# Turning a block's weights ahead of the next block's scores in a two-layer decoder step

## The chip, the cores and the metric

One core of a Trainium2 chip runs the whole program. The metric is the device time of one execution in microseconds, as the median of several runs; lower is better. The engines are TensorE (PE for its matrix products, PEld for its weight loads), VectorE (DVE), ScalarE (ACT), GpSimd (POOL) and SyncE (SP), which issues most transfers.

## What is computed

The reference is one inference step of a two-layer decoder on 1024 prompt rows and 8 single rows with a past of 1024 (the samples). Each layer normalises x, projects it (h @ w_in) into a pooling part and q, k, v of four heads, attends, projects back, and then runs a convolution-gated feed-forward part. What matters here is the attention of the prompt, with two score maps per head:

```python
def diff_core(q, k, v, q_pos, k_pos, lam):
    s = jnp.einsum('bqhcd,bkhcd->bhcqk', q, k).astype(F32) * (HEAD_DIM ** -0.5)
    mask = k_pos[None, :] <= q_pos[:, None]
    s = jnp.where(mask, s, -jnp.inf)
    p = jax.nn.softmax(s, axis=-1)
    a = p[:, :, 0] - lam * p[:, :, 1]
    return jnp.einsum('bhqk,bkhe->bqhe', a.astype(v.dtype), v)
```

HEAD_DIM is 64, a block has 128 queries, and a prompt has 8 blocks.

## The kernel before

The program is written engine by engine; every order of work and every semaphore wait is set by hand, and each engine runs its list in that order. A layer has three stages: the input projections, four heads of attention (about 85 us each, the last one longer), and the feed-forward part.

**A head.** Its eight blocks are taken in the order 7, 0, 6, 1, 5, 2, 4, 3 (`ORDER`), one in each of the steps s = 0 to 7. Block i sees i + 1 blocks of 128 keys, so its two score maps are 128 x 128(i + 1). Narrow and wide blocks alternate: in step s the scores of step s + 1 are made, so the even steps make narrow ones (1, 2, 3 and 4 blocks of keys) and the odd ones wide ones (7, 6, 5, and in step 7 the 8 blocks of the next head).

**Who does what for one block.** PE makes the two score maps in the PSUM banks 2-3 and 4-5 (`scores`, lines 549 to 567: products of 64 rows at L560 and L564, then a causal mask of 128 rows at L566). DVE takes the row maxima (`maxima`, L1930), ACT the two exponentials (`exps`, L1418 and L1421), and DVE puts them together into the weights in SBUF (`combine`, L1939 to L1946), which frees bank 4. PE then turns the weights in rounds of up to four blocks into bank 6 (`turn_p`, L574; a turn is one product of the weights with the identity; two instructions), ACT copies each round to SBUF (`take_p`, L1436), and PE multiplies them by v (`weigh`, L585) into bank 7. The result is squared by ACT (`square`, L1430), POOL makes the factor (`rms`, L1149, L1151), DVE scales by it (`normalise`, L1956), PE turns it into bank 6 (`turn_out`, L596) one step later, and ACT takes it (`take_out`, L1447; L1444 in the last head).

**What fills the gaps.** Between these PE runs products that have no part in the chain: in the first three heads the projections of the next head (`in_slice`, L484), in the last head those of the output (`out_slice`, L499), in the banks 0 and 1 by turns. `FILL` and `FILL_OUT` say how many of them a step has; a third of them stands behind each of the two places in a step, the rest behind `turn_out`. In step 7 a third is 6 products.

**The samples.** Each head also has the 8 samples: POOL multiplies gathered cache pages (L1174) and DVE sums them (`k_sum`, L1971); in step 4 PE turns these sums (L618), in steps 5 and 6 it weighs gathered pages of v (`sample_values`, L642), whose transfers POOL starts (L1166), and in step 7 of the first three heads it spreads the next head's q over the partitions (`spread_q`, L546) through bank 6 and bank 7.

**The order on the other engines in a step.** Neither list is touched by the change:

```python
# ACT, step s                      # DVE, step s
square(it, s - 1)                  maxima(*after)
take_p(it, s, 0)                   normalise(it, s - 1)
exps(*after)                       combine(*after)
...
take_p(it, s, 1)                   k_sum(it, b)
...
take_out(it, s - 1)
```

`after` is the block of the next step. So the exponentials of the next block stand behind the copy of this block's first round on ACT, `take_out` stands behind these exponentials, and `normalise` stands behind the next block's maxima on DVE.

Of the kernel before, what the change touches and what calls it, by code (L numbers as in the profile page):

```python
# [63 lines left out]
def rounds(i):  # L64
    return [list(range(a, min(a + 4, i + 1))) for a in range(0, i + 1, 4)]


def third(s, counts):

    return 0 if counts is FILL_OUT and s == 0 else counts[s] // 3  # L70
# [66 lines left out]
def hybrid_decoder_kernel(nc, x_prompt, x_sample, cache_k, cache_v, state_pool, state_conv, page_table, norm1_g, w_in,  # L137
# [4 lines left out]
    with ExitStack() as ctx:  # L142
# [178 lines left out]
        def claim(pe, name, b):  # L321
            USE[name] = (b, USES[b])
            if USES[b]:
                pe.wait_ge(bank_free[b], USES[b])
            USES[b] += 1
            return b
# [10 lines left out]
        def freed(eng, name):  # L337
            b, n = USE[name]
            eng.wait_ge(bank_free[b], n + 1)
# [76 lines left out]
        def _(pe):  # L416
# [93 lines left out]
            def slices(l, items, banks):  # L510
                for kind, n, t in items:
                    yield from (in_slice if kind == "in" else out_slice)(l, n, t, next(banks))

            def take(fill, n):
                for _ in range(n):
                    next(fill, None)
# [21 lines left out]
            def small_k(it):  # L538
                b = claim(pe, ("ks", it), 6)
                pe.transpose(bank[0:8, b, 0:P], k_buf[it % 2][:, SEQ:T], ident).then_inc(bank_full[b], 1)  # L540
# [8 lines left out]
            def scores(it, s):  # L549
                i = ORDER[s]  # L550
                q, k = q_buf[it % 2], k_buf[it % 2]
                for c in range(2):
                    claim(pe, ("s", it, s, c), 2 + 2 * c)
                if s == 0:
                    pe.wait_ge(roped, it * 2 + 2)
                halves = [(2 + 2 * c, slice(c * HEAD_DIM, (c + 1) * HEAD_DIM)) for c in range(2)]
                for n, at in enumerate(range(0, i * P, 512)):
                    w = min(512, i * P - at)
                    for b, rows in halves:
                        pe.matmul(bank[:, b + n, 0:w], q[rows, i * P:(i + 1) * P], k[rows, at:at + w],  # L560
                                  start=True, stop=True)
                last = [bank[:, b + i // 4, (i % 4) * P:(i % 4 + 1) * P] for b, _ in halves]
                for c, (b, rows) in enumerate(halves):
                    pe.matmul(last[c], q[rows, i * P:(i + 1) * P], k[rows, i * P:(i + 1) * P], start=True, stop=False)  # L564
                for c, (b, rows) in enumerate(halves):
                    pe.matmul(last[c], mask[:, 0, :], mask[:, 1, :], start=False, stop=True  # L566
                              ).then_inc(bank_full[b], 1)

            def turn_p(it, s, r):
                b = claim(pe, ("p", it, s, r), 6)  # L570
                if r == 0:
                    freed(pe, ("s", it, s, 1))
                for n, i in enumerate(rounds(ORDER[s])[r]):
                    ins = pe.transpose(bank[:, b, n * P:(n + 1) * P], probs[s % 2][:, i * P:(i + 1) * P], ident)  # L574
                ins.then_inc(bank_full[b], 1)
# [13 lines left out]
            def turn_out(it, n):  # L589
                b = claim(pe, ("to", it, n), 6)  # L590
                if n == QT_N:
                    freed(pe, ("so", it))
                    pe.transpose(bank[:, b, 0:8], o_norm8, ident[0:8, 0:8]).then_inc(bank_full[b], 1)
                else:
                    freed(pe, ("o", it, n))
                    pe.transpose(bank[:, b, 0:P], o_norm, ident).then_inc(bank_full[b], 1)  # L596

            def turn_v(it, r, b):
                claim(pe, ("vt", it, r), b)
                l, h = it // N_HEADS, it % N_HEADS  # L600
                if r == 0:
                    freed(pe, ("g", l, U_V(h), NT - 1))
                for a in range(4):
                    i = 4 * r + a
                    ins = pe.transpose(bank[:, b, a * P:(a + 1) * P], v_T[:, i * P:(i + 1) * P], ident)
                ins.then_inc(bank_full[b], 1)

            def small_v(it):
                b = claim(pe, ("vs", it), 6)
                pe.transpose(bank[0:16, b, 0:P], v_T[:, SEQ:T + 8], ident).then_inc(bank_full[b], 1)  # L610

            def turn_sample_scores(it):
                for r in range(2):
                    b = claim(pe, ("ss", it, r), 7 - r)
                    if r == 0:
                        pe.wait_ge(k_red, (it + 1) * DEC_BATCH)
                    for a in range(4):
                        ins = pe.transpose(bank[0:16, b, a * P:(a + 1) * P], s_score[:, :, :, 4 * r + a], ident)  # L618
                    ins.then_inc(bank_full[b], 1)
                b = claim(pe, ("ss", it, 2), 7)  # L620
                pe.wait_ge(qk_done, it + 1)
                pe.matmul(bank[0:16, b, 0:1], comp8, ones[:, 0:1], start=True, stop=True).then_inc(bank_full[b], 1)

            def sample_weights(it):
                b = claim(pe, ("sw", it), 6)
                pe.wait_ge(soft_sel, it + 1)
                for j in range(N_PAGES):
                    ins = pe.matmul(bank[:, b, j * 8:j * 8 + 8], soft[:, j * P:(j + 1) * P], sel8,
                                    start=True, stop=True)
                ins.then_inc(bank_full[b], 1)  # L630
# [37 lines left out]
            for l in range(DEPTH):  # L668
# [48 lines left out]
                it = l * N_HEADS  # L717
# [12 lines left out]
                for h in range(N_HEADS):  # L730
                    it = l * N_HEADS + h
                    final = h == N_HEADS - 1
                    if final:
                        fill = slices(l, [("out", m, t) for m in range(KC) for t in range(NT)], banks)
                        counts = FILL_OUT
                    else:
                        fill = slices(l, [("in", u(h + 1), t) for u in (U_K, U_Q, U_V) for t in range(NT)], banks)
                        counts = FILL
                    for s in range(QT_N):
                        part = third(s, counts)  # L740
                        if s + 1 < QT_N:
                            scores(it, s + 1)
                        elif not final:
                            scores(it + 1, 0)
                        turn_p(it, s, 0)
                        take(fill, part)
                        if len(rounds(ORDER[s])) > 1:
                            turn_p(it, s, 1)
                        take(fill, part)
                        if s >= 1:  # L750
                            turn_out(it, s - 1)
                        elif h:
                            turn_out(it - 1, QT_N - 1)
                        if s == 0:
                            turn_v(it, 0, 7)
                            turn_v(it, 1, 6)
                            small_v(it)
                            if h:
                                turn_out(it - 1, QT_N)
                        if s == 4:  # L760
                            turn_sample_scores(it)
                        if s == 5:
                            sample_weights(it)
                            if not final:
                                turn_k(it + 1, 0, 6)
                                turn_k(it + 1, 1, 7)
                        if s == 7 and not final:
                            spread_q(it + 1, 0, 6)
                            spread_q(it + 1, 1, 7)
                            small_k(it + 1)  # L770
                        if final and s == 0:
                            weigh(it, s)
                        if s == 5:
                            sample_values(it, 0)
                        take(fill, counts[s] - 2 * part)
                        if s == 6:
                            sample_values(it, 1)
                        if s == 7:
                            sample_out(it, next(banks))
                        if not (final and s == 0):  # L780
                            weigh(it, s)


                it = l * N_HEADS + N_HEADS - 1
# [1432 lines left out]
```

## Time and profile before

| | us |
|---|---|
| median of 3 runs | 2738.33 |
| their lowest and highest | 2734.73, 2739.3 |
| the profiled execution | 2739.19 |
| its span, first to last instruction | 2737.4 |

The mean granted clock of TensorE in the profiled execution was 0.962 of full speed. The page gives the busy time of each engine, the chain of work that ended last, and groups of instructions; the trace behind it can be asked for waits, for stretches and for single instructions in order of time. Start times count from the first instruction. An instruction's duration on PE runs to its modelled end, so consecutive products overlap: how far their starts lie apart is what they cost.

### The profile page before, as it was taken

The page shows a single profiled execution, that of the slowest core. Times are in us where ns is not written, and L with a number is a line of the kernel's source. Part 1 is how long each engine was busy: PE and PEld are TensorE (multiplying, and loading weights), DVE is VectorE, ACT ScalarE, POOL GpSimd, SP SyncE. Part 2 cuts the span into 40 slices and gives each one's busy share as a digit, 9 for nine tenths or more (in the row PEclk, how much of TensorE's full clock was granted, in tenths as well). Part 3 has the DMA queues.
Part 4 walks back from the last instruction along what each step waited for, and adds up shares of the span by engine and source line. Part 5 has one row for each costly group of instructions (what it writes and reads, how often), then busy time and mean ns, then how long its engine had stood idle before and what let it go on. Part 6 is the DMA issues. An engine that isn't in the chain of part 4 may idle for free.

```text
span 2737.4 us, 41317 instructions
## 1 busy us (share of the span) xinstructions
PE 2545.7 (93%) x16556; PEld 2381.9 (87%) x16556; DVE 1417.5 (52%) x1845; ACT 740.3 (27%) x1409; POOL 794.9 (29%) x537
## 2 busy tenths in 40 slices
PE   6889898989999999999988899899899999999996
PEld 6777777889999999999887777688899999999995
DVE  6554555265454544444565556545455454544445
ACT  3134433242111111111142444424211111111112
POOL 1254555312122212222122566442221122112220
PEclk8999999999999999999999999899999999999998
DMA  4334444201111111111113455421111111111101
GB/s 144 104 102 148 147 143 149 85 25 46 46 46 46 46 46 46 46 46 41 63 40 105 140 153 159 162 82 47 47 47 46 46 46 46 46 46 46 46 23 62
DMA packets 78359, 205.96 MB, mean 75 GB/s; under 512 B 9146, under 2 KB 31100, under 8 KB 77994
## 3 DMA queue, kind: packets, MB, share of 16 engines
q1 hardware_dynamic: 57018, 136.27, 15.0%
q0 software_dynamic: 18496, 67.58, 7.9%
q8 instruction: 67, 1.10, 0.2%
q10 hardware_dynamic: 2752, 0.80, 0.1%
q14 instruction: 26, 0.21, 0.0%
HBM read 176.63 MB, written 19.98 MB: 72 GB/s over the span
## 4 chain that ended last, share of the span: by engine, by line
PE 80%; DVE 8%; issue 4%; ACT 3%; POOL 3%; DMA 2%; ACTq 1%; DVEq 0%; POOLq 0%; SPq 0%
PE bank L820 35%; PE bank L843 19%; PE bank L484 8%; PE bank L499 5%; PE bank L585 2%; PE bank L560 2%; DMA arena<-in_cache_v,idx 1%; PE bank L877 1%; DVE arena L1898 1%; PE bank L642 1%; PE bank L664 1%; POOL arena L1166 1%; PE bank L574 1%; POOL w_lo L1131 1%; DVE arena L1783 1%
## 5 line engine op out<-in xcount | busy, mean ns | idle before, releaser
L1249 POOL TENSOR_TENSOR w_lo<-w_raw,w_hi 128x1024 fp32r<-128x1024 f32 x126 | 309.8, 2459 | 1166.5 <-ACT w_hi L1619 1166.5
L2126 DVE TENSOR_TENSOR resid<-bank,resid 128x1032 f32<-128x1032 f32 x336 | 414.2, 1233 | 94.6 <-PE bank L843 94.6
L820 PE MATMUL bank<-act_hi,w_hi 128*128 128x344 f32 x2016 | 433.8, 324 | 3.7 <-DVE arena L2101 3.7
L820 PE MATMUL bank<-act_hi,w_lo 128*128 128x344 f32 x2016 | 428.2, 321 | 0.0
L820 PE MATMUL bank<-act_lo,w_hi 128*128 128x344 f32 x2016 | 426.8, 320 | 0.0
L820 PEld LDWEIGHTS bank<-act_hi,w_hi 128*128 128x128 f32 x2016 | 336.2, 189 | 7.5 <-issue 3.8
L820 PEld LDWEIGHTS bank<-act_hi,w_lo 128*128 128x128 f32 x2016 | 341.1, 189 | 0.0
L820 PEld LDWEIGHTS bank<-act_lo,w_hi 128*128 128x128 f32 x2016 | 338.4, 189 | 0.0
L843 PE MATMUL bank<-gate_hi,w_hi 128*128 128x344 f32 x1008 | 237.2, 344 | 8.3 <-DVE gate_lo L2119 8.3
L484 PE MATMUL bank<-act_hi,w_hi 128*128 128x344 f32 x672 | 225.6, 336 | 14.2 <-DVE arena L1879 14.2
L484 PE MATMUL bank<-act_hi,w_lo 128*128 128x344 f32 x672 | 225.0, 335 | 0.0
L484 PE MATMUL bank<-act_lo,w_hi 128*128 128x344 f32 x672 | 220.9, 329 | 0.0
L843 PE MATMUL bank<-gate_hi,w_lo 128*128 128x344 f32 x1008 | 214.3, 321 | 0.0
L843 PE MATMUL bank<-gate_lo,w_hi 128*128 128x344 f32 x1008 | 214.1, 321 | 0.0
L1131 POOL TENSOR_TENSOR w_lo<-w_raw,w_hi 128x1024 fp32r<-128x1024 f32 (+1 forms) x56 | 137.2, 2451 | 211.0 <-ACT w_hi L1288 210.8
L843 PEld LDWEIGHTS bank<-gate_hi,w_hi 128*128 128x128 f32 x1008 | 156.3, 190 | 44.0 <-DVE resid L2126 24.1
L1930 DVE TENSOR_REDUCE stat<-bank 128x1 f32<-128x128 f32 (+7 forms) x128 | 90.9, 752 | 197.5 <-PE bank L566 197.5
L1631 ACT ACTIVATE arena<-arena 128x1024 f32<-128x1024 f32 x44 | 46.7, 1062 | 528.0 <-DVE arena L2109 528.0
L843 PEld LDWEIGHTS bank<-gate_hi,w_lo 128*128 128x128 f32 x1008 | 170.0, 189 | 0.0
L843 PEld LDWEIGHTS bank<-gate_lo,w_hi 128*128 128x128 f32 x1008 | 169.9, 189 | 0.0
L2117 DVE TENSOR_TENSOR arena<-bank,arena 128x1032 f32<-128x1032 f32 x44 | 54.4, 1236 | 207.3 <-PE bank L820 207.0
L1174 POOL TENSOR_TENSOR arena<-arena 128x1024 f32<-128x1024 f32 x64 | 152.1, 2381 | 20.8 <-ACT arena L1411 19.4
(238 smaller groups left out, 4032.3 us busy)
## 6 DMA issues: line engine op xcount, KB each, us to landing
w_raw<-in_w_up SPq DMA_DIRECT2D x88, 512.0 KB, 3.9
w_raw<-in_w_down SPq DMA_DIRECT2D x44, 512.0 KB, 3.4
w_raw<-in_w_in SPq DMA_DIRECT2D x32, 512.0 KB, 3.4
out<-arena SPq DMA_DIRECT2D x24, 512.0 KB, 3.3
arena<-arena SPq DMA_DIRECT2D x64, 129.0 KB, 2.4
w_raw<-in_w_out SPq DMA_DIRECT2D x16, 448.0 KB, 3.5
mix_spill<-arena SPq DMA_DIRECT2D x12, 516.0 KB, 3.5
arena<-in_x_prompt SPq DMA_DIRECT2D x8, 512.0 KB, 11.4
```

The source lines that it names most:

```text
L484: ins = pe.matmul(bank[:, b, 0:TW], w_of(w, l, n, k), x[:, k, cols(t)], start=(k == 0 and m == 0), stop=(k == KC - 1 and m == 2))
L499: ins = pe.matmul(bank[:, b, 0:TW], w_of(w, l, U_O + m, c), x[:, c, cols(t)], start=(c == 0 and a == 0), stop=(c == KC - 2 and a == 2))
L560: pe.matmul(bank[:, b + n, 0:w], q[rows, i * P:(i + 1) * P], k[rows, at:at + w], start=True, stop=True)
L585: ins = pe.matmul(bank[:, b, 0:P], a_T[:, r, n * P:(n + 1) * P], v_tok[:, j, :], start=(j == 0), stop=(j == i))
L820: ins = pe.matmul(grp(u[0])[:, t, :], w_of(w, l, n, k), x[:, k, cols(t)], start=(k == 0 and n_ == 0), stop=(k == KC - 1 and n_ == 2))
L843: ins = pe.matmul(grp(u[0])[:, t, :], w_of(w, l, n, m), x[:, cols(t)], start=(n_ == 0), stop=(n_ == 2))
L1131: pool.tensor_tensor(w_lo[:, slot, 0:width], w_raw[:, r % SLOTS, 0:width], w_hi[:, slot, 0:width].bitcast(F32), ALU.subtract).then_inc(w_l ...
L1174: pool.tensor_tensor(kp, kp, q_row, ALU.mult).then_inc(k_mul, 1)
L1249: pool.tensor_tensor(w_lo[:, slot, :], w_raw[:, r % SLOTS, 0:1024], w_hi[:, slot, :].bitcast(F32), ALU.subtract).then_inc(w_lo_done, 1)
L1930: dve.tensor_reduce(stat[:, s % 2, c:c + 1], flat(b)[:, 0:width], AX_X, ALU.min).then_inc(att_bias, 1)
L2117: dve.tensor_tensor(tiles(gate), grp(u[0]), tiles(gate), ALU.mult).then_inc(fg_free[u[0]], 1)
L2126: dve.tensor_tensor(tiles(resid[:, m, :]), grp(u[0]), tiles(resid[:, m, :]), ALU.add).then_inc(fg_free[u[0]], 1)
```

## The change

In each step of a head the call that turns the first round of the current block's weights is moved from behind the next block's scores to in front of them. The two waits that the two calls have in common (the banks of the scores are free, the weights are combined) are the same semaphore; the turn also claims bank 6. In step 7 of a last head no scores follow, and nothing moves. The lists of the other engines stay as they are.

```diff
                     for s in range(QT_N):
                         part = third(s, counts)
+                        turn_p(it, s, 0)
                         if s + 1 < QT_N:
                             scores(it, s + 1)
                         elif not final:
                             scores(it + 1, 0)
-                        turn_p(it, s, 0)
                         take(fill, part)
                         if len(rounds(ORDER[s])) > 1:
                             turn_p(it, s, 1)
```

## Rows read from the trace of the kernel before

**Rows 1.** The page's part 4: shares of the chain that ended last, by engine.

```profile
PE 80%; DVE 8%; issue 4%; ACT 3%; POOL 3%; DMA 2%; ACTq 1%; DVEq 0%; POOLq 0%; SPq 0%
```

**Rows 2.** PE's waits, layer 0's heads: line, releaser, total us, times, longest.

```profile
PE bank L618 <- DVE parts_b L1971: 7.7, 4, 2.1
PE bank L642 <- DMA arena<-in_cache_v,idx: 6.7, 3, 2.3
...
PE bank L546 <- ACT arena L1447: 2.5, 3, 0.8
PE bank L499 <- DVE resid L2001: 2.5, 2, 2.2
...
PE bank L596 <- DVE arena L1956: 1.2, 3, 0.4
```

**Rows 3.** Timeline of step 7, layer 0's first head: start, length, engine, line.

```profile
236.89 1.77 PE L560 MATMUL bank<-arena 64*128 64x512 f32 x8
...
238.94 0.61 PE L574 MATMUL bank<-con,arena 128*128 128x128 f32 x4
239.09 2.36 DVE L1930 TENSOR_REDUCE stat<-bank 128x1 f32<-128x1024 f32 x2 [4.61 <-PE bank L566]
...
240.34 1.11 ACT L1418 ACTIVATE arena<-bank,stat 128x1024 f32<-128x1024 f32 x1 [0.16 <-DVE stat L1930]
...
241.85 0.30 PE L596 MATMUL bank<-con,arena 128*128 128x128 f32 x1 [0.41 <-DVE arena L1956]
...
242.58 0.36 ACT L1447 ACTIVATE arena<-bank,par 128x128 f32<-128x128 f32 x1
...
242.99 1.98 PE L546 MATMUL bank<-arena,con 128*128 128x512 f32 x4 [0.85 <-ACT arena L1447]
```

**Rows 4.** PE's timeline at three places where one kind of product follows another.

```profile
153.36 0.27 PE L540 MATMUL bank<-con,arena 128*8 128x128 f32 x1
153.56 0.70 PE L560 MATMUL bank<-arena 64*128 64x512 f32 x2
...
235.58 1.38 PE L585 MATMUL bank<-arena 128*128 128x128 f32 x10
...
534.15 1.38 PE L585 MATMUL bank<-arena 128*128 128x128 f32 x10
535.37 0.60 PE L574 MATMUL bank<-con,arena 128*128 128x128 f32 x4
```

**Rows 5.** Timeline of step 4, layer 0's first head, from the mask products on.

```profile
198.27 0.29 PE L566 MATMUL bank<-mask 128*128 128x128 bf16 x2
...
198.73 0.19 PEld L484 LDWEIGHTS bank<-act_hi,w_lo 128*128 128x128 f32 x1
...
198.78 1.01 DVE L1930 TENSOR_REDUCE stat<-bank 128x1 f32<-128x384 f32 x2
...
199.04 0.60 ACT L1436 ACTIVATE arena<-bank 128x512 f32<-128x512 f32 x1 [0.93 <-PE bank L574]
...
199.53 0.57 ACT L1418 ACTIVATE arena<-bank,stat 128x384 f32<-128x384 f32 x1
...
199.79 0.14 PEld L574 LDWEIGHTS bank<-con,arena 128*128 128x128 f32 x1
```

**Rows 6.** Timeline of step 0, layer 0's last head.

```profile
419.48 0.49 DVE L1930 TENSOR_REDUCE stat<-bank 128x1 f32<-128x128 f32 x2 [3.85 <-PE bank L566]
...
420.47 0.36 ACT L1418 ACTIVATE arena<-bank,stat 128x128 f32<-128x128 f32 x1
...
424.67 0.48 PE L596 MATMUL bank<-con,arena 128*128 128x128 f32 x1 [3.38 <-ACT arena L1436]
```

**Rows 7.** Stretches: busy us (count) of PE, PEld, DVE, ACT, POOL; TensorE's clock; DMA share, GB/s.

```profile
232.10:235.50 3.40, 3.39 (x64) 2.21 (x64) 2.31 (x4) 0.00 (x0) 0.00 (x0) 0.50 0.02 5
238.90:242.20 3.30, 2.84 (x19) 2.39 (x19) 2.62 (x3) 2.45 (x4) 2.42 (x3) 1.00 0.52 160
242.30:245.70 3.40, 2.71 (x10) 1.58 (x11) 1.84 (x4) 1.90 (x6) 3.26 (x2) 1.00 0.98 324
```

## Prediction

> **What bounds the kernel now.** I read the page's chain first, then PE's waits inside the heads, then the timeline of single steps, and last the stretches with their clock. The chain lies on PE for 80% of the span [rows 1], so a change of PE's order counts only where PE's work grows or where PE waits. The waits show where that is. Inside the heads nothing waits for `combine` except in each layer's very first step, where turn and scores alike wait for it; all later weights are ready before PE comes for them. So what the move does to the turns themselves is worth nothing: they are not late now. What can be late are the five waits of [rows 2]: the samples' sums in step 4 (L618), the cache pages in step 6 (L642), the result turned in step 7 (L596), the spreading of q behind it (L546), and the banks of the output slices in the last head (L499). Each is released by an engine whose list runs through the next block's scores, or through a transfer. The question is which of them start from the scores, since the scores become later.
>
> **How much later the scores come.** Two steps with ten products of `weigh` show it. Where scores follow, they start 236.89 - 235.58 = 1.31 us after the first of the ten [rows 3, 4]; in the last head's step 7, where a turn follows at once, it starts 535.37 - 534.15 = 1.22 us after it [rows 4]. Four turns last 0.61 us from first start to last end, one alone about 0.28, so their starts are (0.61 - 0.28) / 3 = 0.11 us apart [rows 3]. Scores behind a turned block start 153.56 - 153.36 = 0.20 us after it [rows 4]. In the new order scores thus start 1.22 + 3 x 0.11 + 0.20 = 1.75 us after `weigh` starts and not 1.31: **0.44 us later** with four turned blocks, 0.33 with three, 0.22 with two, 0.11 with one. The turn itself comes earlier by the length of the scores. No instruction is added or removed, no transfer is issued in the moved part, and neither SP's nor POOL's list is crossed. The turn's claim of bank 6 is new in that place: the last user of the bank is a step earlier, nearest in step 7, where ACT copies the samples' values while PE still has the 1.31 us of `weigh` to run. I take nothing for it; at most it could take one ACT copy of 0.4 us (the length of L1447) six times, 2.2 us.
>
> **Step 7 of the first three heads (six places): +0.44 each.** Here the scores are the widest and the cover is the shortest, twelve fill products. The chain in [rows 3]: scores, maxima from 239.09 (2.36 us for two), exponentials from 240.34, started by the maxima with ACT idle, so not by the copy in front; `take_out` at 242.58 right behind them; `spread_q` at 242.99 after PE had waited 0.85 us, on top of 0.41 at `turn_out`, which itself waits for `normalise` behind the maxima. Every link starts from the scores, PE already waits, so all 0.44 us are paid: 6 x 0.44 = 2.6 us. Queued behind `spread_q` on PE are the rest of the fill, `weigh` and the next head, which all move with it.
>
> **Step 5 of the last head (two places): +0.33 each.** Of the 2.5 us that the output slices wait in layer 0, 2.2 are in one place and 0.3 in the other [rows 2]. The 0.3 is step 5: DVE adds the slice only behind `combine`, which follows the wide exponentials. Three turned blocks: 2 x 0.33 = 0.65 us. The 2.2 us stand in step 1, where DVE is still summing pages when the scores end, and one turned block (0.11) hides behind that.
>
> **Step 4 (eight places): nothing.** L618 waits for the sums behind `combine` of the block whose scores step 4 makes. Its exponentials start at 199.53, behind the copy that began at 199.04 [rows 5]. In the new order the copy is out of the way early. The scores end at 198.27 + 0.29 + 0.44 = 199.00; the two maxima take 1.01 together, so the first is there at 199.5 and the exponentials start where they start now: two effects of 0.4 us cancel. Its ends: a gain of 0.25 each as in the next part, or a full loss of 0.44.
>
> **Step 0 of the last head (two places): -0.25 each.** PE waits 3.38 us at L596 for a copy that stands behind exponentials and three conversions on ACT [rows 6]. The maxima there are tiny (0.49 for two), and the exponentials start at 420.47 only because the copy is in front. Now the copy is early; maxima begin at 419.48 + 0.44 = 419.92, the first is there 0.25 later, and the exponentials start near 420.2: 2 x 0.25 = 0.5 us back.
>
> **The other steps: no wait, but another neighbour.** In steps 1 and 3 and in the non-final step 5 the delay (0.11 to 0.33) reaches results that PE asks for later. In step 6 it falls between the two halves of the samples' values, where PE waits over 2 us for pages whose transfers started before; that wait takes it up. What changes in every step is what the fill follows: the mask products of the scores, no longer a turn. The trace has no such pair. A turn's load takes 0.14 us, a fill product's 0.19 [rows 5], so from below it costs nothing and by the loads it costs 0.05. From above I take 0.20, the whole start of a new kind in [rows 4]. I take 0.05, as the mask products keep the array at 128 rows as the fill does. It counts where no wait takes it up, 5 steps in six heads less the first step of each layer, and 4 in two heads: 28 + 8 = 36 places, 1.8 us, between 0 and 7.2.
>
> The Trainium skill ("TensorE: Matmul & The Clock Gate", section "Step-by-step: what each phase is for") says that PE pulls weight loads ahead of running products when they go to the array's background buffer; by it the fill's load would be hidden and this term would be 0, a sum of 2.8 us and 2741.1; no run so far has the pair.
>
> **Sum.** 2.6 + 0.65 + 0 - 0.5 + 1.8 = 4.55, say 4.6 us: 2739.19 becomes 2743.8 for the profiled execution. The median of the runs is 0.86 below that execution, so I forecast 2738.33 + 4.6 = **2742.9 us**, 0.17% more. A measurement tells 0.2%, 5.5 us, from no change: below 2732.9 is faster, above 2743.8 slower.
>
> **Rivals.** First, *the longer wait lowers the clock in step 7.* In the stretch around these waits PE is granted the full 2.4 GHz [rows 7]; behind the wait for pages just before, some 2.2 us, it ran at 0.50, that is 1.2 GHz, for the 3.4 us shown [rows 2, 7]. In step 7 PE would idle 0.41 + 0.85 + 0.44 = 1.70 us, between the two. If the clock falls there, 3.4 us at half speed cost up to 1.7 us: six times, 10.2 us, 2753. It decides once the first half-speed stretch follows `spread_q`. Against it: the idle time is split in two. Chance 0.12. Second, *the fill starts badly behind the mask* (0.20 at 36 places): 5.4 us more, 2748. Chance 0.15. Third, *nothing adds up*: PE's delay in step 7 is given back, because the next head's waits start from other engines, or a half-speed stretch like that of 232.1 drops out (1.7 us each, three heads of a layer, 5.1): between 2735 and 2741, around 2738. For it: the runs shown differ by 4.6 us among themselves. Against: each wait after step 7 starts from PE. Chance 0.20. Fourth, *the earlier copy wins*: if ACT's copies and not the maxima hold the narrow steps, step 4 gains 0.25 in eight places, and the fill costs nothing: 2.6 + 0.65 - 2.0 - 0.5 = 0.75, 2739; faster than 2732.9 only if half-speed stretches drop out with it. Chance 0.08. The forecast keeps 0.45, with 2740 to 2746 as its own range.
>
> **How the numbers follow.** Slower by over 0.2%: the two slow rivals (0.27) and the upper part of the forecast's range (0.13), 0.40. Faster: the lowest part of the third and fourth, 0.06. Within: 0.54. The range of 2737 to 2750 leaves out the clock rival's full price and the lower part of the third.
>
> **What would show it.** Right: in step 7 L546 waits near 1.3 us (now 0.85) or its sum with L596 grows by 0.44 in all six heads; L618 keeps its 1.8 to 2.1; the last head's step 5 waits near 0.65; the last head's first `turn_out` 0.25 sooner after the `weigh` of the head before; the first fill product starts 0.05 to 0.1 us later behind L566 than now behind L574. Wrong: L618's wait moving by more than 0.2, a new wait of L574 for bank 6, or a clock of 0.50 behind L546.

## The result and the profile after

The median of ten runs is 2742.68 us, that of the kernel before beside it 2736.53: a ratio of 1.0023, with a 95% interval of 1.0013 to 1.0033, or 6.3 us (3.6 to 9.0). A second set of nine runs of the same kernel gave 2742.86 against 2735.9, 1.0021 (1.0011 to 1.0031). The change is slower by about 0.2%; the forecast was 2742.9. One execution of each kernel (3141.78 us before, 6602.77 after) lies far from all the others and is left out of the ratio. The ratios here and below are formed from the single runs, so they can differ from the quotient of two medians, by up to 0.0008. The profiled execution took 2743.43 us against 2739.19, with a granted clock of 0.962 in both.

The page's part 4 answers to [rows 1]; the chain stays on PE:

```profile
PE 80%; DVE 8%; issue 4%; ACT 3%; DMA 2%; POOL 2%; ACTq 1%; DVEq 0%; POOLq 0%; SPq 0%
```

PE's waits in layer 0's heads, to be held against [rows 2]:

```profile
PE bank L618 <- DVE parts_b L1971: 7.6, 4, 2.1
PE bank L642 <- DMA arena<-in_cache_v,idx: 5.9, 3, 2.1
...
PE bank L596 <- ACT arena L1436: 4.7, 4, 3.8
PE bank L596 <- DVE arena L1956: 3.4, 4, 1.0
PE bank L499 <- DVE resid L2001: 2.8, 2, 2.2
PE bank L546 <- ACT arena L1447: 2.5, 3, 0.8
```

L618 and L546 have not moved. L596 behind `normalise` (L1956) went from 1.2 us in three waits to 3.4 in four, and L499 grew by 0.3. The three waits of step 7 make 1.2 us of the growth (0.80 each for 0.41). The fourth wait, 1.04 us in step 5 of the second head, is not the change's: such waits come and go from one execution to the next, in both orders (last section). So the place is step 7; its timeline in layer 0's first head answers to [rows 3]:

```profile
235.88 1.38 PE L585 MATMUL bank<-arena 128*128 128x128 f32 x10
...
237.10 0.60 PE L574 MATMUL bank<-con,arena 128*128 128x128 f32 x4
...
237.63 1.77 PE L560 MATMUL bank<-arena 64*128 64x512 f32 x8
...
239.83 2.36 DVE L1930 TENSOR_REDUCE stat<-bank 128x1 f32<-128x1024 f32 x2 [5.01 <-PE bank L566]
...
241.09 1.12 ACT L1418 ACTIVATE arena<-bank,stat 128x1024 f32<-128x1024 f32 x1 [2.75 <-DVE stat L1930]
...
242.59 0.30 PE L596 MATMUL bank<-con,arena 128*128 128x128 f32 x1 [0.80 <-DVE arena L1956]
...
243.32 0.36 ACT L1447 ACTIVATE arena<-bank,par 128x128 f32<-128x128 f32 x1
...
243.73 1.98 PE L546 MATMUL bank<-arena,con 128*128 128x512 f32 x4 [0.84 <-ACT arena L1447]
247.86 1.16 PE L585 MATMUL bank<-arena 128*128 128x128 f32 x8
```

The turn stands 1.22 us behind `weigh`, the scores 237.63 - 235.88 = 1.75 (1.31 before), `spread_q` 243.73 - 235.88 = 7.85 (7.41 before). From one `weigh` to the next it is 11.98 us against 11.54: 0.44 more, and every link from the maxima on is late by the same amount. The next `weigh` of the kernel before, to be held against 247.86:

```profile
247.12 0.38 PE L585 MATMUL bank<-arena 128*128 128x128 f32 x1
```

PE's waits at L596 and L546 together are 1.64 for 1.26, so 0.38 of the 0.44 is waiting; by the other 0.05 or so PE gets there later.

Held step against step at equal clock, from the starts of `weigh` in both traces, the rest is small. In the first three heads step 0 is +0.04, step 1 +0.05, step 2 -0.06, step 3 +0.03, step 4 +0.05 (in the middle of the heads; step 2 ranges from -0.02 to -0.09). In the last head steps 2, 3 and 6 are +0.05, +0.04 and +0.03, step 5 waits 0.28 longer, and step 0 is 0.23 shorter. Counted over the layers this is 6 x 0.44 + 6 x 0.11 + 2 x (0.12 + 0.28 - 0.23) = 3.6 us. Steps 4 to 6 of the first three heads hold waits for GpSimd and for cache pages, and the half-speed stretches behind them; single ones differ by up to 1.8 us in both directions. Taken together over the six heads they are 1.2 us shorter than before in this profile and 0.1 shorter in the profile of the second set, so no cost of the change is seen there. One place stands out, step 7 in the last of layer 1's first three heads. Timeline, and stretches (busy us and counts of PE, PEld, DVE, ACT, POOL, then the granted clock):

```profile
1745.76 0.30 PE L596 MATMUL bank<-con,arena 128*128 128x128 f32 x1 [0.80 <-DVE arena L1956]
...
1746.91 2.92 PE L546 MATMUL bank<-arena,con 128*128 128x512 f32 x4 [0.84 <-ACT arena L1447]
```

```profile
1743.00:1746.00 3.00, 2.20 (x14) 1.81 (x12) 2.62 (x3) 1.74 (x3) 2.18 (x3) 1.00 0.78 205
1746.00:1748.00 2.00, 1.16 (x4) 0.58 (x4) 1.23 (x3) 0.85 (x3) 1.97 (x2) 0.95 0.91 295
1748.00:1750.00 2.00, 2.00 (x5) 0.72 (x4) 0.61 (x2) 0.74 (x2) 0.79 (x1) 0.50 0.91 338
```

Behind the same two waits as elsewhere the clock falls to 0.50, 1.2 GHz, in the middle of `spread_q`. That step lasts 13.60 us and not 11.98. This is the first rival, in one of six places. It was hardly an extra cost there: in the other five heads step 6 holds a half-speed stretch of 3.4 us and lasts 11.1 to 11.7 us, in this one it holds none and lasts 9.63, and steps 6 and 7 together are 23.23 us for 23.1 to 23.7. The stretch came one step later.

### The profile page after: what moved, and what is told of

Same layout as the page of the kernel before. It is cut to its first block, busy times and chain, and to the rows that moved or that the text cites. A ratio compares the mean times of both kernels' runs of the same rounds, so it can differ in the third digit from the quotient of the medians.

```text
span 2741.6 us, 41317 instructions
## 1 busy us (share of the span) xinstructions
PE 2549.7 (93%) x16556; PEld 2378.3 (87%) x16556; DVE 1415.3 (52%) x1845; ACT 740.3 (27%) x1409; POOL 794.9 (29%) x537
## 4 chain that ended last, share of the span: by engine, by line
PE 80%; DVE 8%; issue 4%; ACT 3%; DMA 2%; POOL 2%; ACTq 1%; DVEq 0%; POOLq 0%; SPq 0%
PE bank L820 35%; PE bank L843 19%; PE bank L484 8%; PE bank L499 5%; PE bank L585 2%; PE bank L560 2%; DMA arena<-in_cache_v,idx 1%; PE bank L642 1%; PE bank L877 1%; DVE arena L1898 1%; PE bank L574 1%; PE bank L664 1%; DVE arena L1783 1%; ACT arena L1418 1%; POOL w_lo L1131 1%
## 6 DMA issues: line engine op xcount, KB each, us to landing
arena<-in_x_prompt SPq DMA_DIRECT2D x8, 512.0 KB, 11.1
```

## The experiments

The late-chain theory says that the scores of step 7 come 0.44 us later, and everything behind them with it. Its rivals say that every step pays a little, or that the clock pays. The first two kernels split the change in two:

```diff
+                        early = s == QT_N - 1    # second kernel: s < QT_N - 1
+                        if early:
+                            turn_p(it, s, 0)
                         if s + 1 < QT_N:
                             scores(it, s + 1)
...
+                        if not early:
+                            turn_p(it, s, 0)
```

> The turn stands in front of the scores in step 7 of the first three heads alone (six places); all other steps have the old order. Theory of the late chain: all of the cost is here, so L596 in step 7 waits 0.80 us (0.41 before) and L546 0.84 in all six heads, and the time rises by 6 x 0.44 = 2.6 us, ratio 1.0010. Rival, every step pays (a worse start of the scores or the fill): no more than a tenth of the change's 6.2 us, 0.6 us, ratio 1.0002. Rival, half-speed stretches: any change of a head's length moves where TensorE's clock falls, so the time is off by up to 5 us either way with no tie to the six waits.

> The turn stands in front of the scores in every step except step 7. Late chain: no cost in the first three heads, 0.28 us more at L499 in step 5 of the two last heads and about 0.25 us back at L596 in their step 0, so within 0.5 us of the kernel before, ratio 1.0000 to 1.0003. Rival, every step pays: 0.05 us in some 40 places and more, 2 to 4 us, ratio 1.0007 to 1.0015. Rival, half-speed stretches: off by up to 5 us either way.

Step 7 alone gave 2738.0 us against 2735.86, 1.0016 (1.0006 to 1.0027). That is 2.1 us at the medians and 4.4 by the ratio (1.6 to 7.4), where 2.6 was expected. Its profile has +0.42 to +0.54 in all six step 7s and stays within 0.03 of the kernel before in steps 0 to 3 (lines behind the edit are shifted by four):

```profile
238.50 0.30 PE L596 MATMUL bank<-con,arena 128*128 128x128 f32 x1 [0.79 <-DVE arena L1960]
239.64 1.98 PE L546 MATMUL bank<-arena,con 128*128 128x512 f32 x4 [0.84 <-ACT arena L1451]
```

All but step 7 gave 2737.18, 1.0010 (0.9998 to 1.0021), with 11.53 to 11.54 in step 7. The two parts add up to the whole (0.0026 for 0.0021 to 0.0023) and step 7's is the larger, but their intervals overlap widely; what ties the loss to step 7 is the profile.

The next pair gives step 7 more to do while PE waits: eight more fill products there and others moved, in the old order and in the new.

```diff
-FILL = [30, 36, 24, 34, 22, 32, 18, 20]
+FILL = [26, 32, 20, 30, 20, 30, 30, 28]
```

> Old order, but the fill products of the first three heads are shared out anew: 26, 32, 20, 30, 20, 30, 30, 28 in the eight steps for 30, 36, 24, 34, 22, 32, 18, 20. Step 7 has 18 products in front of the turned result for 12 (0.95 us more cover), step 6 more in front of the second half of the samples' values (12 x 0.157 = 1.9 us). Late chain: PE's waits at L596 and L546 in step 7 shrink from 1.25 to about 0.3 us, those at L642 from 2.2 to about 0.3, so some 2.8 us less in each of six heads, 17 us or 0.6% faster, if the steps that gave up products stay covered; if they do not, the wait comes back at L596 or L618 of steps 0 to 5. Rival, the waits are fixed by something that moves with PE's work: no change.

> The change together with the new shares of fill products. Late chain: the scores in step 7 still come 0.44 us later, but with 18 products in front of the turned result the wait of L596 begins later by as much as its releaser, so of the 0.44 us some stay only at L546: between 0 and 2.6 us slower than the old order with the same shares. Rival, every step pays: 2 us or more slower than it even where no wait is left. Rival, half-speed stretches: no fixed difference between the two.

The old order gave 2727.21, 0.9975 (0.9964 to 0.9986); the new one 2731.74, 0.9991 (0.9980 to 1.0001): still 4.5 us apart, with 12.63 us against 12.20 in every step 7. The cover had not hidden the 0.43; in the new order it shows at L546 (1.19 us for 0.84), since L596 no longer waits. Timeline of step 7 in the old order with more cover:

```profile
237.95 1.09 ACT L1421 ACTIVATE bank<-bank,stat 128x1024 f32<-128x1024 f32 x1
238.70 0.27 PE L596 MATMUL bank<-con,arena 128*128 128x128 f32 x1
239.05 0.45 ACT L1362 ACTIVATE arena<-bank 128x344 f32<-128x344 f32 x1
239.39 0.37 ACT L1447 ACTIVATE arena<-bank,par 128x128 f32<-128x128 f32 x1
239.81 1.98 PE L546 MATMUL bank<-arena,con 128*128 128x512 f32 x4 [0.84 <-ACT arena L1447]
```

L596's wait is gone, but the longer fill brought a copy of a finished slice (L1362) between the exponentials and `take_out` (L1447) on ACT, and L546 waits as long as before. That is one reason why the 0.6% expected was too much. The larger one is in the steps that gave products up: in each of the six heads PE now waits 1.2 to 1.3 us at L596 in step 2 and some 0.45 in step 4, where it had hardly waited, and L642 still waits 0.4 to 1.1 us for the 0.3 expected. PE's waits there, layer 0's heads:

```profile
PE bank L596 <- DVE arena L1956: 4.4, 4, 1.3
...
PE bank L642 <- DMA arena<-in_cache_v,idx: 2.5, 3, 1.1
```

A sharper test is to take the chain off the scores. In step 7 of the first three heads `normalise` goes in front of the maxima, and `take_out` in front of the exponentials:

```diff
 # ACT
                         take_p(it, s, 0)
+                        if s == QT_N - 1 and not final:
+                            take_out(it, s - 1)
                         if s + 1 < QT_N or not final:
                             exps(*after)
...
-                        if s >= 1:
+                        if s >= 1 and (s < QT_N - 1 or final):
                             take_out(it, s - 1)
 # DVE
+                        first = s == QT_N - 1 and not final
+                        if first:
+                            normalise(it, s - 1)
                         if follows:
                             maxima(*after)
...
```

> Old order of turn and scores; in step 7 of the first three heads DVE scales the last result ahead of the next head's maxima and ACT takes it ahead of the next head's exponentials, so that PE's two waits there no longer hang on the next head's scores. Late chain: the wait at L596 (0.41 us) goes, L546 waits some 0.46 us for 0.85 (the bare way from the turned result through ACT), the exponentials come about 1.7 us later, which is covered. Six times 0.8 us, so 4.8 us less than the kernel before, ratio 0.9983, half-speed stretches aside (plus or minus 3 us). Rival, the waits in step 7 are not set by the next head's scores: no change.

> The change together with the new order of DVE and ACT in step 7. Late chain: the scores come 0.44 us later as before, but no wait of PE starts from them, so step 7 is as long as in the old order with the same unhooking (within 0.1 us each), and the two kernels differ by only what the other steps cost, about 1 us: ratio to the kernel before 0.9983 to 0.9990. Rival, the 0.44 us are paid on PE itself (a worse order of products): step 7 stays 0.4 us longer in each head, 2.6 us more than the old order unhooked.

The two gave 2736.75 and 2737.21 against 2735.9, both 1.0003 (0.9993 to 1.0014 and 0.9994 to 1.0012). With the chain unhooked the change costs 0.5 us at the medians, less than these runs can tell from nothing, where it costs 6 to 7 with the chain in place on the same chip; and a step 7 at full clock takes 11.46 us for 11.40: of the 0.44 us 0.06 is left. The old order itself gained nothing, where 4.8 us were expected; one wait made room for another. PE and ACT in step 7, old order unhooked:

```profile
239.40 0.27 PE L596 MATMUL bank<-con,arena 128*128 128x128 f32 x1
239.71 0.37 ACT L1447 ACTIVATE arena<-bank,par 128x128 f32<-128x128 f32 x1 [1.40 <-PE bank L596]
239.97 1.11 ACT L1418 ACTIVATE arena<-bank,stat 128x1024 f32<-128x1024 f32 x1
240.12 1.98 PE L546 MATMUL bank<-arena,con 128*128 128x512 f32 x4 [0.46 <-ACT arena L1447]
...
242.81 0.27 PE L540 MATMUL bank<-con,arena 128*8 128x128 f32 x1 [0.70 <-ACT arena L1411]
```

L596 no longer waits and L546 waits 0.46, but the copies of the spread q (L1411) now stand behind the exponentials, and L540 waits 0.70 for its bank: 1.16 us in all for the 1.26 before.

Then the larger wait, that for the cache pages in step 6 (L642), was attacked with twelve products moved to it from step 0. It ran with and without the unhooking, and in the new order; the change was also timed once more:

```diff
-FILL = [30, 36, 24, 34, 22, 32, 18, 20]
+FILL = [18, 36, 24, 34, 22, 32, 30, 20]
```

> Old order, step 7 unhooked, and 12 fill products moved from step 0 (30 to 18) to step 6 (18 to 30), in front of the second half of the samples' values, where PE waits 2.2 us for pages; the other steps keep their shares, since POOL's products on the pages set the pace from step 1 to step 4. Late chain: 6 x 0.8 us as in the old order unhooked and 6 x 1.9 us at L642, 16 us less, ratio 0.994; if step 0 has no room for it, its waits (L574, L596) take some back. Rival, the pages' transfers start from PE's arrival and move with it: only the 4.8 us.

> The changed kernel as it is, beside the others on one chip. Counted by equal steps of its profile it costs 6 x 0.44 in step 7, 2 x 0.28 at L499, some 0.6 in the small steps and gives 2 x 0.23 back: 3.3 us, ratio 1.0012. Rival, half-speed stretches add to it in every run: 6 us, ratio 1.0022.

> The kernel before with twelve of step 0's thirty fill products moved to step 6 (18 in step 0, 30 in step 6), and nothing else. If the gain of the run that also unhooked step 7 (0.9929) was this shift alone, this gives 0.993 as well, since unhooking alone gave 1.0003; PE's wait for the cache pages (L642, three waits of about 2.2 us in layer 0) falls to about 0.7 each, 9 us over six heads in half steps and more in what follows. Rival: the two edits need each other, and this gives only half, 0.9965.

> The changed order with the same shift of twelve fill products from step 0 to step 6. By the late chain of step 7 the change costs here what it costs on the old sharing, since step 7 keeps its twelve products in front of the chain: 0.44 us in six places and about 0.7 for the rest, 3.3 to 6 us over the run beside it, a ratio of 0.9945 if that one is at 0.993. Rival: the cost comes from how the slower step 7 meets the half-speed stretch behind the wait for pages in step 6; with that wait shorter the two orders would agree within 1.5 us.

Moved and unhooked: 2716.92 against 2735.9, 0.9929 (0.9916 to 0.9943). Moved alone: 2714.75 against 2732.55, 0.9931 (0.9919 to 0.9944), so the move accounts for the whole gain, and none is seen from the unhooking. It beats both kernels. PE's waits there, layer 0's heads:

```profile
PE bank L642 <- DMA arena<-in_cache_v,idx: 1.3, 2, 0.7
```

L642 waits 1.3 us for the 6.7 of [rows 2], and the half-speed stretch of 3.4 us behind it drops out of step 6 in all six heads (one of them had none before): with it that step took 11.5 to 11.9 us, now it takes 9.5 to 10.1 although it holds twelve products more. Step 0, with twelve fewer, is 1.9 us shorter.

The repeat is the 1.0021 told above, nearer to the rival's 1.0022 than to the 1.0012 of the count. And on the new sharing the change costs more: 2722.37, 0.9963 (0.9951 to 0.9976), 7.6 us over the old order. Its profile has 11.98 us in four step 7s and 13.66 in two. Timeline and stretches in one of those two:

```profile
317.87 0.30 PE L596 MATMUL bank<-con,arena 128*128 128x128 f32 x1 [0.80 <-DVE arena L1956]
319.02 3.45 PE L546 MATMUL bank<-arena,con 128*128 128x512 f32 x4 [0.85 <-ACT arena L1447]
```

```profile
318.00:320.00 2.00, 1.15 (x3) 0.60 (x3) 1.12 (x3) 0.96 (x3) 1.98 (x2) 0.85 0.75 274
320.00:322.00 2.00, 2.00 (x3) 0.47 (x3) 0.72 (x2) 0.60 (x1) 1.17 (x1) 0.50 0.95 371
```

`spread_q` takes 3.45 us for 1.98. The two stretches are 1.7 us each, and with the 3.6 of the count they come to 7.0 of the 7.6 us; here step 6 has no half-speed stretch in either order, so nothing is saved in exchange. So on this sharing the change was tried without step 7's wait, in two ways: with the unhooking, and with the turn first in every step but step 7 (both edits as above).

> The changed order, with step 7 unhooked (its normalise and take_out ahead of the maxima and exponentials) and twelve fill products moved from step 0 to step 6. On that sharing the change alone cost 7.6 us (2714.75 against 2722.37); its profile showed 0.44 us in each step 7 and in two of the six heads a half-speed stretch of 3.4 us there (13.66 us for 11.98). If all of that comes from PE's longer wait in step 7, unhooking takes it away: about 0.7 us over the same kernel in the old order (0.9929), a ratio of 0.993, and no half-speed stretch in step 7. Rival: the half-speed stretches come with the new order whatever step 7 waits for, and it stays at 0.995 or above.

> The sharing with twelve products moved from step 0 to step 6, and the turn first in every step but step 7. By the same theory step 7 keeps the old 11.54 us in six heads at full clock and the rest costs about 0.7 us: a ratio of 0.9934 where the old order alone gave 0.9931 and the whole change 0.9963. Rival: the new order brings its cost into other steps on this sharing, and it comes out halfway or worse, 0.995.

They gave 2719.22 and 2716.91 against 2734.09: 0.9943 (0.9929 to 0.9956) and 0.9938 (0.9924 to 0.9952). No step 7 in either profile has a half-speed stretch; each takes 11.45 to 11.46 and 11.53 to 11.55 us. Both lie nearer to the old order's 0.993 than to the change's 0.9963, but the first stands between them and the intervals touch: that most of the 7.6 us is step 7's is what they speak for, not that all of it is.

## Why the prediction held, and where not

**The delay of the scores.** 0.44 us was predicted from three start-to-start distances, and 0.44 was found, at 1.75 us behind `weigh`. The place where it shows was half wrong: L596 took all of the growth, L546 none. A chain that is late as a whole adds to the first wait that it meets; the second starts from there and keeps its length. The sum of both waits grew by 0.38 (1.64 for 1.26) and not by the 0.44 given as a sign, because PE itself arrives at L596 some 0.05 us later; the step as a whole grew by 0.44. The new claim of bank 6, taken at nothing, cost nothing: no first round of turns waits for the bank.

**Step 7, six times 0.44.** Shown: alone it costs 0.44 a place in the profile, and 2.1 us at the medians or 4.4 by the ratio in the runs; without the chain 0.06 a place is left; more products in front do not hide it.

**The last head.** Step 5 waits 0.61 us where 0.65 was predicted. This is PE's row, and behind it the row of before:

```profile
505.62 0.42 PE L499 MATMUL bank<-act_hi,w_hi 128*128 128x344 f32 x1 [0.61 <-DVE resid L2001]
```

```profile
504.38 0.43 PE L499 MATMUL bank<-act_hi,w_hi 128*128 128x344 f32 x1 [0.33 <-DVE resid L2001]
```

In step 0 the first `turn_out` starts 425.23 - 418.49 = 6.74 us after the `weigh` of the head before, against 424.67 - 417.70 = 6.97: the 0.25 was 0.23. These are the rows of after, and behind them the `weigh` of before ([rows 6] has its `turn_out`):

```profile
418.49 1.16 PE L585 MATMUL bank<-arena 128*128 128x128 f32 x8
...
425.23 0.47 PE L596 MATMUL bank<-con,arena 128*128 128x128 f32 x1 [3.75 <-ACT arena L1436]
```

```profile
417.70 1.16 PE L585 MATMUL bank<-arena 128*128 128x128 f32 x8
```

Its wait has grown from 3.38 to 3.75 while the step became shorter, because PE gets there sooner: its wait of 0.69 us for bank 6, at the second round of turns in front of it, is down to 0.10 now that the first round is copied early. A longer wait is not by itself a loss.

**Step 4.** L618 is unmoved, as argued, and so is the start of the exponentials; this timeline answers to [rows 5]:

```profile
197.20 0.60 PE L585 MATMUL bank<-arena 128*128 128x128 f32 x4
...
198.31 0.60 ACT L1436 ACTIVATE arena<-bank 128x512 f32<-128x512 f32 x1
...
199.02 0.29 PE L566 MATMUL bank<-mask 128*128 128x128 bf16 x2
199.09 0.19 PEld L484 LDWEIGHTS bank<-act_hi,w_lo 128*128 128x128 f32 x1
199.12 0.40 PE L484 MATMUL bank<-act_hi,w_lo 128*128 128x344 f32 x1
199.29 1.02 DVE L1930 TENSOR_REDUCE stat<-bank 128x1 f32<-128x384 f32 x2
...
199.89 0.58 ACT L1418 ACTIVATE arena<-bank,stat 128x384 f32<-128x384 f32 x1 [0.98 <-DVE stat L1930]
```

The `weigh` of before, from which its exponentials at 199.53 count:

```profile
196.88 0.60 PE L585 MATMUL bank<-arena 128*128 128x128 f32 x4
```

The exponentials start 2.69 us after `weigh`, 2.65 before; the copy (L1436) is out of their way, and they now wait for the maxima. Two effects of 0.4 us cancel. The fourth rival, that this would be a gain, fell.

**The fill behind the mask.** This term was mis-sized and its reason was wrong. 36 x 0.05 = 1.8 us was counted; the steps without a wait gave 6 x 0.11 + 2 x 0.12 = 0.9. The fill does not start badly: its first load runs at 199.09 beside the mask products and its first product starts 0.03 us after the second of them, as it does behind a turn; the sign given for this term, a start 0.05 to 0.1 later, did not come. Start to start, the old order has 0.205 from `weigh` to the scores, 0.056 from mask to turn and 0.028 from turn to fill; the new one 0.112 from `weigh` to the turn, 0.203 from turn to scores and 0.028 from mask to fill: 0.34 for 0.29. So the 0.05 that single steps show is the turn's and not the fill's: it costs 0.11 behind `weigh` where it cost 0.06 behind the mask, and the other two starts keep their length. Step 2 gains 0.06 because a short wait at `turn_out` shrinks there (L596 starts 1.35 to 1.42 us behind the first of the eight fill products in front of it, 1.44 to 1.53 before); why that result comes earlier is not shown.

The Trainium skill ("TensorE: Matmul & The Clock Gate", section "Step-by-step: what each phase is for") says that PE pulls a weight load ahead of running products when it goes to the array's background buffer. By that the fill's load is hidden, and the load at 199.09 agrees: it runs beside mask products that end at 199.31. The first fill product does start 0.24 us before the next, where later ones are 0.16 apart, but so it does behind a turn: the two orders pay the same. The second rival, *the fill starts badly*, fell.

**The clock.** The first rival was given 0.12 as a whole, all six places at 1.7 us. A clock of 0.50 behind L546 was named as a sign of being wrong, and it came in one place of six in the profile of the change, in none of the second set or of step 7 alone: 1 of 18. As a cost it was small there: step 6 had gone without its own stretch, and the two steps together were no longer than in the other heads. On the new sharing it came in two places of six and cost 3.4 us, since step 6 has no stretch there to make up for it.

What ties the places together is the step before. A half-speed stretch began in step 7 only where step 6 had held none: in 3 of 7 such places with the changed step 7 and its waits of 0.80 and 0.84 us (1 with the change, 6 on the new sharing), in 0 of 15 with the old step 7 and its 0.41 and 0.85 (before, all but step 7, both on the new sharing). In the 17 places of the changed step 7 where step 6 had held one, none began. Why 3 of the 7 and not the other 4 is open.

**The total.** The third rival, *nothing adds up*, fell: both intervals of the ratio leave out 1. The forecast of 2742.9 lies 0.2 us from the median of 2742.68, and that much agreement is luck. The difference forecast was 4.6 us, the runs say 6.3 (3.6 to 9.0) and the count of steps 3.6, with the term of the other steps twice too large; and the forecast started from the median of three runs, 2738.33, where ten gave 2736.53. The two errors, 1.7 us too little and 1.8 too much, cancel. What is shown is the mechanism, with its 2.6 us in step 7, and that the whole loss lies between 3 and 9 us.

Open is what lies between 3.6 and 6.3 us. The runs do not demand it: the count lies at the edge of the first interval and inside the second (3.0 to 8.5). A candidate is that the old step 7 lets PE through steps 6 and 7 without any half-speed stretch more often. On the old sharing that happened in 5 of 24 places with the old or the unhooked step 7 (four profiles), for some 1 to 2 us less each, and in 0 of 18 with the changed one; 6 x 5/24 places at 1 to 2 us make an estimate of 1.3 to 2.5 us an execution. So few places do not show it.

## What to carry to other kernels

Before moving work in front of a producer, find the step where the consumer already waits and follow that chain back: if every link starts from the producer, the whole delay is paid there, and it is paid at the first wait. Moving filler into a step may bring its own copies into the chain, and unhooking one copy may hold up the next, so read the list of every engine again after each move. The larger gain stood beside the change: filler moved from a step whose waits did not grow by it into one that waited for a transfer (0.7%), since it removed most of a wait and the slow clock behind it together. Moved from steps that needed it, in the run with more cover, it let new waits in.

## What the runs showed of the hardware

A small VectorE instruction can last as long as a GpSimd one beside it. In the kernel before the 16 x 8 instruction of `soft_weights` takes 0.28 us in one head; in another it starts 0.11 us behind a GpSimd subtraction and ends with it, 2.29 us later. `normalise` (L1956) stands behind it, and L596 waits in step 5 of such heads: 0.83 and 1.10 us before, 1.04 twice after. The fourteen profiles hold this instruction 112 times. In 71 a GpSimd subtraction was running when it started and had more than 0.25 us to go; each of these 71 ended 0.02 to 0.03 us behind the subtraction, after 0.30 to 2.29 us. In the other 41, where none was running or it was about to end, it took 0.28. The rows, in the two heads:

```profile
501.42 0.28 DVE L1993 TENSOR_SCALAR small<-con,small,lam 16x8 f32<-16x8 f32 x1
```

```profile
1545.80 2.37 POOL L1131 TENSOR_TENSOR w_lo<-w_raw,w_hi 128x1024 fp32r<-128x1024 f32 x1
...
1545.91 2.29 DVE L1993 TENSOR_SCALAR small<-con,small,lam 16x8 f32<-16x8 f32 x1
```

The Trainium skill ("GPSIMD Engine Reference", section "1. Specifications") says that GpSimd shares its SBUF interfaces with VectorE, and that VectorE's instructions in a two-port mode or with two SBUF inputs contend with it. The joint ends agree with that; no run here shows which of the two conditions this instruction meets.

And the clock fell to 0.50 behind two waits of 0.80 and 0.84 us with 1.15 us between their ends, in three of 24 places (four profiles); in all three the step before had held no half-speed stretch. Behind waits of 0.41 and 0.85, in 24 places of four profiles, no half-speed stretch began in the step.
